# Two transformer blocks on one core: narrow weight operands laid side by side, gates and hidden layers interleaved with the queries, and three moves in VectorE's order

## The chip, the cores and the metric

One Trainium2 chip, one of its cores. The metric is the device time of one execution in microseconds (us), of which the profile covers the span from the first to the last instruction. All inputs and outputs are float32.

## The reference

Two blocks over 256 tokens of width 1024, batch 1, one after the other. What matters here is the first part of each.

```python
n = rmsnorm(h, g_mix)                       # 256 x 1024
proj = n @ w_in                             # b, c, h_conv, q, six k/v of 256 columns, g_br (48), g_conv, g_attn
k_cmp = compress(kvh(k_c), pos_k, w1_k, w2_k, n_cmp)   # n_cmp = 15 windows of 32 tokens, stride 16
v_cmp = compress(kvh(v_c), pos_v, w1_v, w2_v, n_cmp)
...
def compress(kv, pos, w1, w2, n_cmp):
    blk = kv[:, idx] + pos                  # 4 heads x 15 windows = 60 rows of 32 * 64 values
    return gelu(blk @ w1) @ w2              # 60 x 2048 by 2048 x 256, then 256 x 64
...
o = einsum('bsch,cbshd->bshd', sigmoid(g_br).reshape(B, S, 3, 16), [o_cmp, o_sel, o_win])
mix = sigmoid(g_conv) * y_conv + sigmoid(g_attn) * (o @ w_attn_out)
h = h + mix @ w_o
h = h + (silu(n @ w_gate) * (n @ w_up)) @ w_down       # D_FF = 2816
```

The second block has differential attention with a relative bias, a gated linear attention and a pooling part. Its `proj` has 16 columns `g_lr`, from which `z = g_lr @ gla_gate_w + gla_gate_b` gives the decays.

## The kernel before, in words

**Split precision.** The large matmuls take operands of type fp32r. Each operand is split in a high part (a copy by ScalarE into that type) and a low part (VectorE, operand minus high part), and a product is the sum of high by high, high by low and low by high. Activations lie in `AA` (128 partitions x 20 chunks x 2 x 256; `AH` its high and `AL` its low half). Weights come in 120 *units* of up to 1 MB (list `units`, L210 to L270).

**The ring of units.** SyncE's queue loads unit i into `RAW[i % 4]` as soon as the low part of unit i - 4 is made (L338 to L351). `hi(i)` on ScalarE (L511 to L520) writes `HI[i % 3]` in two halves, once the unit has landed and TensorE is done with unit i - 3. `lo(i)` on VectorE (L939 to L944) writes `LO[i % 3]`. TensorE waits for the halves with `unit_ready` (L1449). All four orders are written out by hand, and each engine does its instructions strictly in the order in which they stand.

**Calls of TensorE.** `stationary` (L1455 to L1473) has 128 columns of a unit as the stationary operand and 256 tokens moving: three matmuls (L1471) for each of 8 slices of 128. `both` (L1475) and `moving` (L1497) are forms for the feed-forward part and for token-major results. `take(bank, sem, value)` makes TensorE wait until the PSUM bank's last result has been read.

**First part** (L1541 to L1627). Keys, the two block units (k_c, v_c, whose results VectorE lays out as 16 slices of 60 columns, `block_sums`, split again by `block_high` and `block_low` into `BLOCKS`), the 48 gate columns (U_GATES, unit 3; `stationary` with n=48 into B[2]), four query units of two calls each (units 4 to 7), and then the hidden layers of both compressions (L1592 to L1605, units 8 to 11, three matmuls L1603 for each of 16 slices, with 60 columns). ScalarE takes the tanh of the gates from B[2] (L571) and TensorE turns them by two transposes (L1590); VectorE scales them into `GATE` (L1021). The gelu of a hidden layer runs on 60 partitions x 256: square (L589), cubic factor (L1031, L1033), tanh (L591), product (L1035), and then two transposes (L1610) and a copy into `HT` (L595). After those come the value unit 12, the products with w2 (L1617, L1622) and a small product for the relative bias (L1627).

**Attention of the first block** has 26 steps (`steps`, L281 to L288; 9 for the first 128 tokens with four heads in a step, 17 for the others with two). In step i TensorE does `scores(i)`, one or two calls of the *filler* (`FILL_AT`, L300), `turn_weights(i - 1)` (L1661) and `outputs(i - 2)` (L1698). The filler is a generator on each engine that gives the rest of the first block's projections piece by piece: a second set of keys and values, the convolution (L1110 to L1125 on VectorE), the gates of conv and attention, and the products with w_conv_out (L1138). ScalarE does `exponents(i)` (L630), the filler, `turned_weights(i - 1)` (L641), `taken` (L647). VectorE does `most(i)` (the maxima, L1062), the filler, `weights(i)` (four instructions, the last is L1083), and `taken` (L1089).

**Second block.** Unit U_TWO+4 is loaded with 128 columns, of which 16 are used (`feature_major(U_TWO + 4, 0, 1, 0)`), `LR` is copied from them (L823) and multiplied with `GW` (16 partitions, L1921). On VectorE `second_most` (L1329, L1332) waits for a turn of TensorE before its third use, and `lo(U_TWO + 9)` stands behind it (L1374, L1375). TensorE uses that unit in `rows(U_TWO + 9, ...)`, after `second_turn(1)`.

Of the kernel before, what the change touches and what calls it, by code (L numbers as in the profile page):

```python
# [6 lines left out]
F32 = mybir.dt.float32  # L7
# [3 lines left out]
ALU = mybir.AluOpType  # L11
# [48 lines left out]
def program(nc, A, out):  # L60
    with ExitStack() as ctx:
# [3 lines left out]
        def sem(name):  # L65
# [40 lines left out]
        GW = sb("GW", [16, 128])  # L106
        PW = sb("PW", [128, 2, 64])
        ROOT = sb("ROOT", [128, 8])
        hmask = sb("hmask", [128, 256])
        B = [ctx.enter_context(nc.psum_tensor(f"B{i}", [128, 512], F32)) for i in range(8)]  # L110
# [3 lines left out]
        BLOCKS = [AA[:, 12 + 4 * kv:16 + 4 * kv, :, :].rearrange("p c a n -> p (c a n)").rearrange("p (a n) -> p a n", a=2)  # L114
                  for kv in range(2)]
# [33 lines left out]
        FIRST_IN, SECOND_IN = 80, 48  # L149
# [20 lines left out]
        gates_pe, gates_tanh, gturn_pe, gates_sb = sem("gates_pe"), sem("gates_tanh"), sem("gturn_pe"), sem("gates_sb")  # L170
        q_pe, q_sb = sem("q_pe"), sem("q_sb")
        hid_pe, hid_act, hid_dve = sem("hid_pe"), sem("hid_act"), sem("hid_dve")
        hturn_pe, hturn_sb = sem("hturn_pe"), sem("hturn_sb")
# [57 lines left out]
        cols(w1, GBO, 48, gates_pe, 1)  # L231
        for u in range(4):
# [3 lines left out]
        for kv, n in enumerate(("cmp_w1_k", "cmp_w1_v")):  # L236
            for i in range(2):
                units.append((A[n][0].rearrange("(t p) n -> p t n", p=128)[:, 8 * i:8 * i + 8, :], 8, 256,
                              hid_pe, 2 * kv + i + 1))
# [21 lines left out]
        cols(w2in, 2048, 128, fm_pe, 1)  # L261
# [14 lines left out]
        U_KEYS, U_BLOCK, U_GATES, U_Q, U_HID, U_VALS = 0, 1, 3, 4, 8, 12  # L276
# [28 lines left out]

        def pieces(ring, size, i, k):

            src, nk, n, _, _ = units[i]
            if len(src.shape) == 4:
# [49 lines left out]
        def _(e):  # L359
# [22 lines left out]
            for i, n in ((47, "q_norm_g_2"), (48, "k_norm_g_2"), (50, "gla_norm_g_2")):  # L382
                for a in range(2):
# [13 lines left out]
                            pattern=[[128, 2], [-16, 32]], channel_multiplier=1).then_inc(setup, 1)  # L397
            e.memset(KC[:, :, :], 0.0).then_inc(setup, 1)
            e.memset(VB, 0.0).then_inc(setup, 1)
# [15 lines left out]
            e.dma_start(GW[:, :], A["gla_gate_w_2"][0]).then_inc(second_in, 16)  # L415
# [90 lines left out]
        def _(e):  # L506
# [55 lines left out]
            def block_high(kv, src):  # L562
                e.wait_ge(block_sb, 2 * kv + 2)
                e.activation(BLOCKS[kv][:, 0, 0:960], flatten(src[:, 0:4, :])[:, 0:960], ACT.Copy).then_inc(block_hi, 1)
# [8 lines left out]
            for u in range(4):  # L573
                c, jj = u // 2, u % 2
                if u > 0:
                    hi(U_Q + u + 2)
# [1488 lines left out]
```

## Time and profile before

| | |
|---|---|
| median of 3 runs | 765.71 us (765.52 to 767.38) |
| profiled execution, its own time | 765.83 us |
| its span | 764.1 us, 12619 instructions |
| TensorE's granted clock | 1.0 of full speed in every stretch |
| ScalarE / VectorE / GpSimd busy | 421.9 / 521.4 / 68.9 us |
| DMA | 131.78 MB, mean 172 GB/s |

Engines are named PE (TensorE matmul), PEld (its weight load, which overlaps), DVE (VectorE), ACT (ScalarE), POOL (GpSimd) and SP (SyncE). A row of a timeline has the start, the length, the engine, the line of kernel.py, the operation and its tiles, the shapes (out<-in; for a matmul, 128*48 is 128 rows by 48 columns of the stationary operand, then the moving operand), and how many instructions were merged. Matmuls are pipelined, so the length of one (0.28 us) says less than the distance between the starts of two. In brackets stands the idle time before an instruction and what ended it.

### The profile page before, as it was taken

To read this page: it belongs to the slowest core of one execution; us is meant where nothing else is said; L and a number is where in the kernel's file an instruction comes from. 1 tells how busy PE (TensorE), PEld (TensorE's weight loads), DVE (VectorE), ACT (ScalarE), POOL (GpSimd) and SP (SyncE) were. 2 spreads that over 40 slices of the span, in tenths; PEclk is the share of its full clock that TensorE was granted. 3 is DMA by queue.
4 is the path that set the end of the run, shared out by engine and by line. 5 is a ranking of instruction groups with operands and counts; after the bars stand their busy time and mean duration, and the time that the engine had idled before them with its cause. 6 is when DMAs were issued, how large, how long until landed. Compare 5 with 4: busy or idle time off the path is not lost.

```text
span 764.1 us, 12619 instructions
## 1 busy us (share of the span) xinstructions
PE 753.8 (99%) x5057; PEld 668.6 (88%) x5057; DVE 521.4 (68%) x848; ACT 421.9 (55%) x807; POOL 68.9 (9%) x106
## 2 busy tenths in 40 slices
PE   8999999999999999999999999999999999999998
PEld 7999898889899988888888888998888888888886
DVE  5857576786665767887457757888568777447762
ACT  6456656556554546555445646697645655445640
POOL 7200000001011000350000004400100000000000
PEclk9999999999999999999999999999999999999999
DMA  9978446344335556756755662843453665655611
GB/s 279 305 233 269 113 75 188 107 119 157 112 112 193 166 178 197 212 184 213 227 166 176 209 192 61 259 152 116 162 165 116 216 192 195 210 175 168 207 68 55
DMA packets 108398, 131.78 MB, mean 172 GB/s; under 512 B 4317, under 2 KB 97563, under 8 KB 108340
## 3 DMA queue, kind: packets, MB, share of 16 engines
q1 hardware_dynamic: 105780, 126.04, 52.0%
q0 software_dynamic: 2272, 4.42, 2.6%
q8 instruction: 40, 0.66, 0.4%
q10 hardware_dynamic: 288, 0.52, 0.2%
q14 instruction: 18, 0.15, 0.1%
HBM read 129.13 MB, written 1.84 MB: 171 GB/s over the span
## 4 chain that ended last, share of the span: by engine, by line
PE 83%; DVE 10%; ACT 4%; issue 2%; DMA 1%; SPq 0%; POOL 0%; ACTq 0%; DVEq 0%; POOLq 0%
PE B L1510 28%; PE B L1487 21%; PE B L1471 15%; PE B L1492 11%; DVE LO L943 3%; ACT HI L520 2%; ACT PR L630 1%; DVE SM L1062 1%; PE B L1698 1%; DVE PR L1083 1%; PE B L1651 1%; PE B L1569 1%; PE B L1661 1%; PE B L1517 1%; DMA X<-in_x 1%
## 5 line engine op out<-in xcount | busy, mean ns | idle before, releaser
L943 DVE TENSOR_TENSOR LO<-RAW,HI 128x1024 fp32r<-128x1024 f32 (+1 forms) x240 | 284.0, 1219 | 144.8 <-ACT HI L520 144.4
L520 ACT ACTIVATE HI<-RAW 128x1024 fp32r<-128x1024 f32 (+1 forms) x240 | 237.9, 1040 | 57.6 <-PE B L1510 56.8
L1487 PE MATMUL B<-AA,HI 128*128 128x512 f32 x704 | 243.3, 398 | 0.5 <-DVE AA L949 0.5
L1510 PE MATMUL B<-HI,AA 128*128 128x512 f32 (+1 forms) x832 | 217.0, 346 | 1.8 <-DVE LO L943 1.7
L1492 PE MATMUL B<-AA,LO 128*128 128x256 f32 x704 | 183.2, 281 | 0.0
L1471 PE MATMUL B<-AA,HI 128*128 128x256 f32 (+1 forms) x928 | 171.3, 286 | 0.0
L1510 PEld LDWEIGHTS B<-HI,AA 128*128 128x128 f32 x832 | 146.0, 189 | 22.1 <-issue 3.1
L1487 PEld LDWEIGHTS B<-AA,HI 128*128 128x128 f32 x704 | 126.7, 188 | 25.1 <-issue 1.1
L1471 PEld LDWEIGHTS B<-AA,HI 128*128 128x128 f32 (+1 forms) x928 | 143.7, 190 | 4.1 <-issue 2.5
L1510 PE MATMUL B<-LO,AA 128*128 128x512 f32 (+1 forms) x416 | 143.2, 344 | 0.0
L1492 PEld LDWEIGHTS B<-AA,LO 128*128 128x128 f32 x704 | 132.9, 189 | 8.2
L1471 PE MATMUL B<-AA,LO 128*128 128x256 f32 (+1 forms) x464 | 131.1, 283 | 0.0
L1471 PEld LDWEIGHTS B<-AA,LO 128*128 128x128 f32 (+1 forms) x464 | 88.2, 190 | 0.0
L1510 PEld LDWEIGHTS B<-LO,AA 128*128 128x128 f32 x416 | 78.8, 189 | 9.3
L630 ACT ACTIVATE PR<-B,SM 128x128 f32<-128x128 f32 (+1 forms) x64 | 26.2, 418 | 45.3 <-DVE SM L1062 45.3
L745 ACT ACTIVATE SGC<-SGC 128x256 f32<-128x256 f32 x44 | 16.7, 418 | 27.7 <-DVE SGC L1219 27.6
L756 ACT ACTIVATE AA<-SGC 128x256 fp32r<-128x256 f32 x44 | 16.7, 418 | 27.3 <-DVE SGC L1229 27.3
L739 ACT ACTIVATE SGC<-B 128x256 f32<-128x256 f32 x44 | 15.7, 372 | 24.1 <-PE B L1487 24.1
L750 ACT ACTIVATE SGC<-B 128x256 f32<-128x256 f32 x44 | 15.7, 371 | 20.8 <-PE B L1487 20.8
L1214 DVE TENSOR_TENSOR SGC<-B,SGC 128x256 f32<-128x256 f32 x44 | 17.7, 419 | 9.0 <-ACT SGC L739 9.0
L1224 DVE TENSOR_TENSOR SGC<-B,SGC 128x256 f32<-128x256 f32 x44 | 17.7, 419 | 5.4 <-ACT SGC L750 5.4
L1062 DVE TENSOR_REDUCE SM<-B 128x2 f32<-128x512 f32 (+1 forms) x24 | 16.4, 685 | 6.9 <-PE B L1654 6.9
(297 smaller groups left out, 624.4 us busy)
## 6 DMA issues: line engine op xcount, KB each, us to landing
RAW<-in_w_in SPq DMA_DIRECT2D x29, 1024.0 KB, 5.7
RAW<-in_w_gate SPq DMA_DIRECT2D x22, 1024.0 KB, 5.4
RAW<-in_w_up SPq DMA_DIRECT2D x22, 1024.0 KB, 5.4
RAW<-in_w_down SPq DMA_DIRECT2D x22, 1024.0 KB, 5.0
RAW<-in_w_in SPq DMA_DIRECT2D x11, 512.0 KB, 7.1
RAW<-in_w_attn_out SPq DMA_DIRECT2D x4, 1024.0 KB, 5.4
RAW<-in_w_o SPq DMA_DIRECT2D x4, 1024.0 KB, 5.0
RAW<-in_w_out SPq DMA_DIRECT2D x4, 1024.0 KB, 5.2
```

Of the source, the lines that this page charges most:

```text
L520: e.activation(pieces(HI, NSPL, i, k), pieces(RAW, NRAW, i, k), ACT.Copy).then_inc(split_hi, 1)
L630: x = e.activation(PR[:, k, j * w:j * w + w], sc[:, j, :], ACT.Exp, bias=SM[:, 3 * q, j:j + 1], accum_out=SM[:, 3 * q + 1, j:j + 1])
L745: e.activation(SGC[:, f % 4, :], SGC[:, f % 4, :], ACT.Silu).then_inc(silu_sb, 1)
L756: e.activation(AH[:, 8 + f % 12, :], SGC[:, f % 4, :], ACT.Copy).then_inc(ff_hi, 1)
L943: e.tensor_tensor(pieces(LO, NSPL, i, k), pieces(RAW, NRAW, i, k), pieces(HI, NSPL, i, k), ALU.subtract).then_inc(split_lo, 1)
L1062: e.tensor_reduce(SM[:, 3 * q, 0:n], SCORE[q][:, :].rearrange("p (j n) -> p j n", j=n), AX.X, ALU.max, negate=True).then_inc(most_sb, 1)
L1214: e.tensor_tensor(SGC[:, f % 4, :], B[c][:, 0:S], SGC[:, f % 4, :], ALU.add).then_inc(fg_sb, 1)
L1224: e.tensor_tensor(SGC[:, 4 + f % 4, :], B[5 + c][:, 0:S], SGC[:, 4 + f % 4, :], ALU.add).then_inc(fu_sb, 1)
L1471: x = e.matmul(dst, w[:, t, c0:c0 + n], a, start=(t == 0 and k == 0), stop=(t == nk - 1 and k == 2))
L1487: return e.matmul(dst[:, :], hi[:, t, c0:c0 + 128], flatten(AA[:, ch + t, :, :]), start=(t == 0), stop=(t == nk - 1))
L1492: x = e.matmul(dst[:, 0:S], lo[:, t, c0:c0 + 128], AH[:, ch + t, :], start=False, stop=False)
L1510: x = e.matmul(dst, a, w[:, t, c0:c0 + n], start=(first and t == 0 and k == 0), stop=(last and t == nk - 1 and k == 2))
```

## The change

It does the following.

- *Side by side.* For units with fewer than 64 columns (gates, 48, and U_TWO+4, now loaded with 16) the low part is written next to the high part in `HI` (64 columns apart), and `narrow` multiplies 64 + n columns with `AH` and n columns with `AL`: 16 matmuls in place of 24. `BLOCKS` has its high and low parts side by side in the same way, so a hidden layer takes two matmuls for a slice: 124 columns by the high part of w1, 60 columns by its low part.
- *Sums in the turn.* The two halves of such a result lie on different partitions. `summed_turn` multiplies by `SUMS` (two identities one above the other), which turns and adds. The gates' tanh comes after the turn, and so does the whole gelu (on 128 x 120, straight into `HT`; the factor 0.5 moves into later copies). `GW` lies twice on 80 partitions, so that its product adds the two halves.
- *Order of the first part.* The copy of the gates out of B[2] stands right behind hi(4), ahead of hi(5) and block_high(1). The hidden layers stand between the query calls, with their units in that order (q 4, 7, 10, 11; w1 5, 6 and 8, 9), and the values come last. Banks: hidden layers in B[3] and B[4], their turns in B[5] and B[6], the products with w2 in B[2] and B[7].
- *VectorE.* In attention `weights(i)` stands ahead of the filler. `lo(U_TWO + 9)` stands ahead of `second_most(2)`. `block_low(1)` stands behind lo(5) and lo(6).
- *GpSimd.* Three more memsets, one add for `SUMS`, and one more small DMA for `GW`.

```diff
@@ units
+        U_Q, U_HID = (4, 7, 10, 11), (5, 8)
...
-        cols(w2in, 2048, 128, fm_pe, 1)
+        cols(w2in, 2048, 16, fm_pe, 1)
+        def beside(i):
+            return HI[i % NSPL][:, 0:1024].rearrange("p (t a n) -> p t a n", a=2, n=64)
@@ gpsimd
+            e.memset(GW[:, :], 0.0).then_inc(pads, 1)
+            e.tensor_tensor(SUMS[:, :], ident[:, 0:64], ident[:, 64:128], ALU.add).then_inc(pads, 1)
@@ scalar
             block_high(0, SGC)
             hi(4)
+            e.wait_ge(gates_pe, 1)
+            e.activation(TMP[0:112, 0, 0:S], B[2][0:112, 0:S], ACT.Copy).then_inc(gates_act, 1)
+            hi(5)
             block_high(1, SGA)
-            hi(5)
-            e.wait_ge(gates_pe, 1)
-            e.activation(TMP[0:48, 0, 0:S], B[2][0:48, 0:S], ACT.Tanh, scale=0.5).then_inc(gates_tanh, 1)
...
+            hi(6, 0)
+            queries(0, 0)
+            hi(6, 1)
+            queries(0, 1)
+            e.wait_ge(gturn_pe, 1)
+            e.activation(GATE[:, :, :, :].rearrange("p t c h -> p (t c h)"), B[6][:, 0:96], ACT.Tanh, scale=0.5).then_inc(gates_act, 1)
+            hi(7)
+            hi(8)
+            hidden(0)
+            hi(9)
+            queries(1, 0)
+            hidden_square(0)
+            queries(1, 1)
+            hidden_tanh(0)
+            hi(10)
+            hi(11)
+            hidden(1)
...
@@ vector
             block_sums(1, SGA, 1)
-            block_low(1, SGA)
             lo(5)
             lo(6)
+            block_low(1, SGA)
             lo(7)
...
                 if i < NSTEP:
                     most(i)
+                if i < NSTEP:
+                    weights(i)
                 for _ in range(FILL_AT[i]):
                     next(filler)
-                if i < NSTEP:
-                    weights(i)
...
             second_weights(1)
+            lo(U_TWO + 9)
             second_most(2)
-            lo(U_TWO + 9)
             second_weights(2)
@@ tensor
+            def narrow(i, n, dst):
+                unit_ready(i, 1)
+                w = beside(i).rearrange("p t a n -> p t (a n)")
+                for t in range(8):
+                    if t > 0:
+                        e.matmul(dst[0:n, 0:S], w[:, t - 1, 0:n], AL[:, t - 1, :], start=False, stop=False)
+                    if t == 7:
+                        e.matmul(dst[0:n, 0:S], w[:, t, 0:n], AL[:, t, :], start=False, stop=False)
+                    x = e.matmul(dst[0:64 + n, 0:S], w[:, t, 0:64 + n], AH[:, t, :], start=(t == 0), stop=(t == 7))
+                return x
...
+                        if not last:
+                            e.matmul(B[3 + kv][0:124, 0:256], blocks[:, l, 0:124], wh[:, t, :], start=(l == 0), stop=False)
+                        x = e.matmul(B[3 + kv][0:60, 0:256], blocks[:, l, 0:60], wl[:, t, :], start=False, stop=False)
...
+            def summed_turn(dst, src, n, columns):
+                return e.matmul(dst, src[0:64 + n, columns], SUMS[0:64 + n, 0:n], start=True, stop=True)
...
+            queries(0, 0)
+            queries(0, 1)
...
+            hidden(0)
+            queries(1, 0)
+            hidden_turn(0)
+            queries(1, 1)
+            hidden(1)
+            queries(2, 0)
+            hidden_turn(1)
+            queries(2, 1)
...
+            queries(3, 0)
...
+            queries(3, 1)
+            for t in range(2):
+                values(U_VALS, 0, t)
```

## Rows read from the trace of the kernel before

**Rows 1.** The page, part 1: busy us (share of the span) and instructions of each engine.

```profile
PE 753.8 (99%) x5057; PEld 668.6 (88%) x5057; DVE 521.4 (68%) x848; ACT 421.9 (55%) x807; POOL 68.9 (9%) x106
```

**Rows 2.** The page, part 4: the chain that ended last, shares of the span.

```profile
PE 83%; DVE 10%; ACT 4%; issue 2%; DMA 1%; SPq 0%; POOL 0%; ACTq 0%; DVEq 0%; POOLq 0%
```

**Rows 3.** Waits of TensorE, whole span: total us, times, longest us.

```profile
PE B L1661 <- DVE PR L1083: 1.9, 3, 0.9
...
PE B L1510 <- DVE LO L943: 1.7, 1, 1.7
```

**Rows 4.** Timeline of TensorE, the gates' call: start, us, engine, line, operation, count.

```profile
30.49 0.28 PE L1471 MATMUL B<-AA,LO 128*128 128x256 f32 x1
...
30.62 0.40 PE L1471 MATMUL B<-AA,HI 128*48 128x256 f32 x2
...
33.37 0.40 PE L1471 MATMUL B<-AA,HI 128*128 128x256 f32 x2
```

**Rows 5.** Timeline of TensorE, first and last record of the 96 of L1603.

```profile
56.84 0.28 PE L1603 MATMUL B<-HI,AA 128*60 128x256 f32 x1
...
67.97 0.28 PE L1603 MATMUL B<-HI,AA 128*60 128x256 f32 x1
```

**Rows 6.** Timeline of TensorE, the low-rank call.

```profile
495.14 0.40 PE L1471 MATMUL B<-AA,HI 128*128 128x256 f32 x2
...
495.50 0.40 PE L1471 MATMUL B<-AA,HI 128*128 128x256 f32 x2
```

**Rows 7.** Timeline of TensorE, the gates' turns and the W2K product.

```profile
39.01 0.28 PE L1471 MATMUL B<-AA,LO 128*128 128x256 f32 x1
...
39.22 0.32 PE L1590 MATMUL B<-ident,TMP 48*128 48x48 f32 x2
...
39.81 0.28 PE L1471 MATMUL B<-AA,LO 128*128 128x256 f32 x1
...
74.90 0.55 PE L1617 MATMUL B<-HT,W2K 128*128 128x60 f32 x4
```

**Rows 8.** Busy us of each engine, stretch 30 to 40, clock, DMA share, GB/s.

```profile
30.00:40.00 10.00, 10.00 (x85) 9.81 (x84) 8.80 (x13) 4.96 (x7) 0.00 (x0) 1.00 0.91 248
```

**Rows 9.** Timeline of ScalarE and VectorE, query units, with idle before and releaser.

```profile
45.53 0.38 ACT L581 ACTIVATE QT<-B 128x256 f32<-128x256 f32 x1 [2.49 <-PE B L1471]
...
46.89 2.36 DVE L943 TENSOR_TENSOR LO<-RAW,HI 128x1024 fp32r<-128x1024 f32 x2 [2.56 <-ACT HI L520]
```

**Rows 10.** Timelines of three engines, attention steps around 115 to 122 us.

```profile
114.69 0.68 DVE L1062 TENSOR_REDUCE SM<-B 128x4 f32<-128x512 f32 x1
...
116.80 2.01 ACT L520 ACTIVATE HI<-RAW 128x1024 fp32r<-128x1024 f32 x2
...
117.90 1.23 DVE L943 TENSOR_TENSOR LO<-RAW,HI 128x1024 fp32r<-128x1024 f32 x1 [2.52 <-ACT HI L520]
...
120.89 0.69 DVE L1083 TENSOR_TENSOR PR<-PR,SM 128x512 f32<-128x512 f32 x1
...
121.50 0.68 DVE L1089 TENSOR_TENSOR AA<-B,AA 128x512 fp32r<-128x512 f32 x1
...
121.64 0.66 PE L1661 MATMUL B<-ident,PR 128*128 128x128 f32 x4 [0.86 <-DVE PR L1083]
...
122.24 0.65 PE L1698 MATMUL B<-PT,VV 128*64 128x256 f32 x4
```

**Rows 11.** Timelines of VectorE and TensorE, near 195 us.

```profile
194.52 0.41 DVE L1138 TENSOR_TENSOR SGC<-B,SGC 128x256 f32<-128x256 f32 x1
...
195.43 0.40 PE L1471 MATMUL B<-AA,HI 128*128 128x256 f32 x2
```

**Rows 12.** Timelines of VectorE and TensorE, second block, near 527 us.

```profile
524.36 0.69 DVE L1329 TENSOR_TENSOR SGC<-B,QT 128x512 f32<-128x512 f32 x1 [1.89 <-PE B L1875]
...
527.01 2.35 DVE L943 TENSOR_TENSOR LO<-RAW,HI 128x1024 fp32r<-128x1024 f32 x2
...
529.50 0.36 PE L1510 MATMUL B<-HI,AA 128*128 128x256 f32 x1 [1.72 <-DVE LO L943]
```

More of the change, by code:

```diff
@@ L1592, in _ @@
-            for kv in range(2):
-                hi, lo = BLOCKS[kv][:, 0, :], BLOCKS[kv][:, 1, :]
-                take(kv, hid_dve, 2 * kv + 2)
+            def narrow(i, n, dst):
[8 more added lines that the diff above has]
+                return x
@@ L1595, in _, with queries, hidden @@
+            take(2, gates_act, 1)
+            narrow(U_GATES, 48, B[2]).then_inc(gates_pe, 1)
+            def queries(u, k):
+                take(k, q_sb, 2 * u + k + 1)
+                stationary(U_Q[u], 128 * k, B[k][:, 0:S], 0, True).then_inc(q_pe, 1)
+            def hidden(kv):
                 e.wait_ge(block_lo, kv + 1)
+                take(3 + kv, hid_act, 3 * kv + 1)
+                blocks = BLOCKS[kv].rearrange("p l a n -> p l (a n)")
                 for half in range(2):
-                    i = U_HID + 2 * kv + half
@@ L1598, in _ @@
-                    unit_ready(i, 1)
+                    i = U_HID[kv] + half
                     wh, wl = view(HI, i), view(LO, i)
                     for t in range(8):
-                        c = slice(60 * (8 * half + t), 60 * (8 * half + t) + 60)
-                        for k, (a, w) in enumerate(((hi, wh), (hi, wl), (lo, wh))):
-                            x = e.matmul(B[kv][0:60, 0:256], a[:, c], w[:, t, :], start=(half == 0 and t == 0 and k == 0),
-                                         stop=(half == 1 and t == 7 and k == 2))
@@ L1605, in _ @@
-                    x.then_inc(hid_pe, 1)
-            for kv in range(2):
-                e.wait_ge(hid_dve, 2 * kv + 2)
-                take(5 + kv, hturn_sb, kv + 1)
+                        if t % 4 == 0:
+                            unit_ready(i, t // 4)
+                        l, last = 8 * half + t, half == 1 and t == 7
+                        if not last:
+                            e.matmul(B[3 + kv][0:124, 0:256], blocks[:, l, 0:124], wh[:, t, :], start=(l == 0), stop=False)
+                        x = e.matmul(B[3 + kv][0:60, 0:256], blocks[:, l, 0:60], wl[:, t, :], start=False, stop=False)
@@ L1614, in _ @@
+            hidden_turn(0)
+            queries(1, 1)
+            hidden(1)
+            queries(2, 0)
+            hidden_turn(1)
+            queries(2, 1)
+            e.wait_ge(hid_dve, 2)
             e.wait_ge(first_in, FIRST_IN)
-            take(0, ck_sb, 2)
+            take(2, ck_sb, 2)
             for c in range(2):
-                x = e.matmul(B[0][:, 0:60], W2K[:, c, :], HT[:, 0, c, :], start=(c == 0), stop=(c == 1))
+                x = e.matmul(B[2][:, 0:60], W2K[:, c, :], HT[:, 0, c, :], start=(c == 0), stop=(c == 1))
@@ L1624, in _ @@
             x.then_inc(cv_pe, 1)
+            queries(3, 1)
+            for t in range(2):
+                values(U_VALS, 0, t)
             e.wait_ge(setup, FAR)
@@ L1915, in _ @@
             qk_turn(0)
-            feature_major(U_TWO + 4, 0, 1, 0)
+            take(0, lr_act, 1)
+            narrow(U_TWO + 4, 16, B[0]).then_inc(fm_pe, 1)
             feature_major(U_TWO + 5, 0, 2, 4)
```

155 lines of the change are left out of this document (78 added, 77 removed).

## The prediction

> **What bounds the kernel.** I read the page's busy shares first, then its chain, the waits of TensorE, and the timelines where the diff acts. TensorE is busy for 753.8 of 764.1 us [rows 1], and the chain that ended last is 83% TensorE [rows 2]. So a matmul removed is worth its full spacing, and anything else is worth only the idle time of TensorE that it ends: 10.3 us in all, of which 1.9 us are waits of the attention turns L1661 for VectorE's weights L1083, and 1.7 us one wait of L1510 for a low part [rows 3]. VectorE and ScalarE have time to spare on average, but they run one behind the other (high part, then low part, then TensorE), so their order can still make TensorE wait.
>
> The durations are those of the profiled execution: 765.83 us, of which 764.1 are its span. The median of the runs is 765.71, so I subtract 0.1 at the end. A difference under about 0.3% (2.3 us) can't be told from none in this kernel.
>
> **1. Fewer matmuls for narrow operands.** A product costs three matmuls per slice now: high by high, high by low, low by high. The change puts the high and low parts of the narrow operand in one stationary load of 112, 80 or 124 columns; two matmuls per slice remain, one wide and one narrow, both still 256 columns long on the moving side.
> - Gates (U_GATES): the call runs from 30.62 to 33.37, 2.75 us for 24 matmuls, so 0.115 us each with 48 columns; the next call, with 128, steps by 0.12 us (0.24 for two) [rows 4].
> - Hidden layer (L1603): from 56.84 to 68.09 (the last starts at 67.97 and takes one more step), 11.25 us for 96 matmuls of 60 columns, 0.117 us each [rows 5].
> - Low rank (U_TWO+4): 24 matmuls with 128 columns. Three of its matmuls take 0.36 us (495.14 to 495.50), so 2.88 us [rows 6].
>
> Together 16.88 us for 144 matmuls. After: 16 + 64 + 16 = 96. The new wide loads of 80 to 124 columns are shown by no row; the nearest lie on both sides, 48 columns at 0.115 and 128 at 0.120 us. That gives 11.0 to 11.5 us; half of the 96 are of each kind, so I take 0.118, 11.3 us. Gain 5.5 us (5.4 to 5.9).
>
> **2. Turns that also add the two parts.** Six turns of 48 or 60 rows become ordinary f32 matmuls. Such a call leaves two records (W2K: two in the source, four records, 0.55 us together, of which about half is the length of the last, so about 0.1 us each) [rows 7]: six more records, 0.65 us. The present turns pay for something else: from the last matmul before the gates' turns (39.01) to the third after them (39.81) are 0.80 us. Three matmul steps are 0.36, so the two turns cost 0.44 us, though two records of 0.1 would be 0.2; the step before them alone is 0.21 where 0.12 is usual [rows 7]. With 112 or 124 rows that change of shape is gone, and four records of 0.1 are 0.4 us: I take 0 (-0.7 to +0.7). Likewise the one small matmul of the gates' weights with 80 rows in place of 16: -0.1.
>
> **3. The new order ahead of attention.** TensorE has no idle time here; the row for 30 to 40 us shows 10.00 of 10.00 busy [rows 8]. What is to be checked is whether splits and transfers still arrive. By the durations of the rows (high part of a unit 2.0 us, low part 2.36 us [rows 9, 10]) I walked the new order. Gates end at 32.5 in place of 33.4 and their copy, moved ahead of hi(5), holds that back until 32.9; lo(5) ends at 37.4, lo(6) at 39.8, block_low(1) at 41.0, the first half of lo(7) at 42.2. TensorE wants units 5, 6 and 7 at 38.9, 40.8 and 42.7. Unit 10 is ready at 52.3 for 52.9. So the thinnest margins are 0.4 and 0.6 us, and no wait. Of the hidden layers' chains, copy, turn, square, cubic, tanh and product, each step lies beside a query call of 2.9 us. If this cover fails, the old chain tells the price: waits of 0.1 us then, up to one split half (1.2 us) for each of two layers. Two waits of 0.1 us near 71.7 and 75.5 go: -0.2 (-0.2 to +2.4). SP's queue sees 64 KB in place of 512 KB for the low-rank unit and one small transfer more from POOL, whose memsets and add end long before 38 us: nothing. ScalarE and VectorE lose about 2 us of splits, behind TensorE: nothing.
>
> **4. Weights ahead of the fill, 26 steps.** Now VectorE does, in each step, the maxima, then the fill (which often waits for ScalarE's high part), then the weights. In the step at 114.69 the maxima end at 115.4, the exponentials at 116.80, the low part waits until 117.90, the product L1083 comes at 120.89 and TensorE starts at 121.64, after 0.86 us [rows 10]. Moved up, weights begin at 116.9 and end at 118.1, about when the low part could start anyway: in a step that begins a unit the move is free. In the next step the high part is already there; now the low part runs beside the exponentials, then it would wait for them (1.4 us, or less with two of them in place of four) and for the weights (1.2 us). Two steps cost VectorE 9.0 us before and 9.2 after: the same rate, but the fill's own products come about 2.5 us later in every second step, and these free the banks B0 and B1. Queued behind the wait are also taken(), at 121.50 now, which lets TensorE's outputs start at 122.24, and the products L1138. Walking through it: at 122.24 TensorE gains only 0.4 of the 0.86 us, since taken() ends at 121.8; the second gating product of the first round frees its bank near 126.7, 0.5 us late; the two other waits of the three [rows 3], 0.9 and 0.2 us, go. Near 195 L1138 (now at 194.52, needed by 195.43 [rows 11]) comes at 196.2 to 196.6: 1.15 us of new wait. The sum is -0.4 + 0.5 - 0.9 - 0.2 + 1.15, near zero; since TensorE's new waits give slack back to what follows, I take -0.3. Bounds: -1.9 if nothing new waits, +3 if each of the eight fills that free a bank in such a step costs 0.6 us and the old waits still go.
>
> **5. lo(U_TWO+9) ahead of second_most(2).** VectorE is idle for 1.89 us until 524.36, takes the maxima, and only then splits (527.01 to 529.36), while TensorE waits 1.72 us until 529.50 [rows 12]. The split now fits into that idle time: 522.5 to 524.8. The maxima come 0.5 us later and what they feed, the third exponentials and the high part behind them, is wanted well after 530. The wait goes: -1.7 (-1.7 to -1.2, if the copy of UP behind ScalarE is late by that 0.5).
>
> **Sum.** -5.5 - 0.1 - 0.2 - 0.3 - 1.7 = -7.8 us; 765.83 - 7.8 = 758.0, less 0.1 for the median, rounded to **758.0 us**.
>
> **A rule against part 1.** The row: going from 128 to 48 columns at 30.49 to 30.62 costs no more than a usual step, and back neither [rows 4]; going from 128 to 48 rows and back costs 0.24 us beyond the turns' own 0.2 [rows 7]. The Trainium skill, page TensorEngine Tiling (Array Packing), section Key Properties, says that a change of tiling mode, unlike a change of tile, drains TensorE. By that rule, if narrow loads counted as another mode, each alternation would pay; the trace shows it for rows and not for columns.
>
> **Rivals.**
> - *Drain at each alternation* (slower). Place: inside the two narrow calls and the two hidden layers. Wide and narrow loads alternate 14 + 14 + 30 + 30 = 88 times; at 0.12 us (half of the 0.24 above) that is 10.6 us, so 768.6. It decides from 0.09 us per change, where it eats all 7.8. Against it: the two changes of column count in [rows 4]; for it: they are two, and never alternated. This is the case that the rule of the skill describes. Chance 0.03.
> - *VectorE's new waits exceed those that go* (part 4 at its upper bound): 758.0 + 3.3 = 761.3. For it: VectorE's loop is as slow as TensorE's in the convolution steps, and banks are freed from within the fill. Chance 0.15.
> - *The move pays in full*, -1.9 in place of -0.3: 756.4. For it: TensorE's own slack may hide late banks. Chance 0.12.
> - *A split is late ahead of attention* (part 3, upper bound): 760.6. The margins of 0.4 us speak for it, the 0 us of idle now against it. Chance 0.12.
> - *The removed matmuls don't shorten the stretch*: the DMA share is 0.91 from 30 to 40 us [rows 8], and the gain of 4.5 us up to there turns into waits for units 9 to 12; only parts 4, 5 and the low-rank call remain, near 763.0. Against it: high parts waited for TensorE, 2.49 us, not for the transfer [rows 9]. Chance 0.05.
>
> **Numbers.** The forecast has 0.53. The range, 756.0 to 761.5, takes in the three neighbours with the bounds of parts 2 to 4. Faster by over 0.3%: 0.92; within: 0.05 (the rival without shortening and several late ones at once); slower: 0.03.
>
> **What would show it.** L1603's successor has 64 records over about 7.6 us, the two narrow calls 16 each over 1.9 us, steps within stay at 0.12. Scores of attention begin near 73 in place of 77.3. No wait at the call of U_TWO+9. Waits of L1661 for L1083 vanish; in their place small ones for L1089, L1123 or L1138. Wrong if steps in the narrow calls reach 0.2 us, or TensorE waits over 1 us in total between 35 and 73, or over 3 us between 75 and 225.

## The result, and the profile after

The changed kernel takes 761.76 us in the median of 13 runs (760.41 to 764.76), the kernel before 765.87 in as many (765.22 to 769.31). The ratio is 0.9943, with a 95% interval from 0.9927 to 0.996. It is faster, by 4.1 us; the forecast was 7.8 us, and the time lies 0.3 us above the range. The profiled execution took 764.64 us with a span of 762.9, so it is one of the long ones, and the spans must be taken apart before they are compared.

The page, part 1, of the changed kernel (compare [rows 1]):

```profile
PE 752.9 (99%) x5015; PEld 668.0 (88%) x5015; DVE 519.9 (68%) x848; ACT 421.4 (55%) x808; POOL 71.0 (9%) x111
```

There are 42 matmul records fewer: 48 matmuls less, six records more for the summed turns. But TensorE is busy only 0.9 us less: two stretches at half its clock, shown below, keep it busy longer. Its waits have changed as well. The waits of TensorE in the changed kernel (engine, line, releaser: total us, times, longest; compare [rows 3]):

```profile
PE B L1513 <- DVE SGC L1180: 1.9, 1, 1.9
PE B L1778 <- DVE AA L1131: 1.6, 2, 0.8
PE B L1513 <- DVE CG L1165: 1.1, 2, 0.7
```

The attention turns' waits for the weights (1.9 us) and the wait for the low part of U_TWO+9 (1.7 us) are gone. Five others stand in attention, 4.6 us together. L1180, L1131 and L1165 are the old L1138, L1089 and L1123: the gating of the products with w_conv_out, the low part of the outputs in `taken`, and the convolution's gating product.

**Cutting the span.** The transpose of VR ahead of the first block matmuls is a good zero, as TensorE's work up to it is the same in all kernels here. The tile views of that transpose, first of the kernel before and then of the changed one (its first and last start, the same for one record, stand ahead of the semicolon):

```profile
L1575 PE MATMUL B<-ident,VR x1: 260/260/260, 18.8 to 18.8; 51*128 51x51 f32 x1
```

```profile
L1617 PE MATMUL B<-ident,VR x1: 260/260/260, 21.3 to 21.3; 51*128 51x51 f32 x1
```

It comes 2.45 us later in the changed kernel's profile, for no reason of the change: by the trace's clock records TensorE's granted clock rose to full at 4.04 us there and at 12.56 us here. In the other profiles below it rose anywhere from 4.17 to 13.4 us, whichever kernel they are of. The same 26 matmuls ahead of the transpose, before and after, show what the lower clock costs:

```profile
6.18 3.17 PE L1523 MATMUL B<-ones 128*128 128x128 f32 x26
```

```profile
6.94 5.83 PE L1565 MATMUL B<-ones 128*128 128x128 f32 x26
```

(The profile's windows print 1.00 there too; the 1.0 "in every stretch" of the table before holds from the clock's rise on.) From the transpose to the end are 745.3 us before and 741.63 after. Stage by stage, by the starts of the first or last record of a kind:

| from, to | before | after | difference | forecast |
|---|---|---|---|---|
| transpose of VR, first scores | 58.46 | 53.71 | -4.76 | parts 1 to 3 without the low rank: -4.75 |
| first scores, last attention output | 156.27 | 160.42 | +4.15 | part 4: -0.3 |
| on to the second block's first q/k turn | 260.37 | 260.35 | 0 | 0 |
| on to the low-rank product with GW | 6.72 | 5.59 | -1.13 | low-rank call and GW: -1.1 |
| on to the band's first matmul | 31.91 | 29.98 | -1.93 | part 5: -1.7 |

Four stages of five are as forecast. The miss is attention.

**The side-by-side operands.** The changed kernel's lines of TensorE from 33 to 36 us, and by form from 40 to 56 us (rows by columns of the stationary operand, the moving operand, count, then busy us and mean ns):

```profile
L1632 PE MATMUL B<-AA,HI 128*112 128x256 f32 x8 | 1.9, 276 | 0.0
...
L1629 PE MATMUL B<-AA,HI 128*48 128x256 f32 x7 | 1.6, 276 | 0.0
...
L1656 PE MATMUL B<-LO,AA 128*60 128x256 f32 x32 | 7.4, 279 | 0.0
L1655 PE MATMUL B<-HI,AA 128*124 128x256 f32 x30 | 7.2, 283 | 0.0
```

All are there (the last narrow load of the gates' call and the last wide one of each hidden layer stand on lines of their own, L1631 and L1658), and no idle time in front. The timeline of the gates' call and of its turns gives the spacing:

```profile
33.06 0.28 PE L1632 MATMUL B<-AA,HI 128*112 128x256 f32 x1
33.18 0.28 PE L1629 MATMUL B<-AA,HI 128*48 128x256 f32 x1
...
34.88 0.40 PE L1513 MATMUL B<-AA,HI 128*128 128x256 f32 x2
...
40.52 0.28 PE L1513 MATMUL B<-AA,LO 128*128 128x256 f32 x1
40.64 0.54 PE L1663 MATMUL B<-SUMS,TMP 112*128 112x48 f32 x4
41.00 0.36 PE L1655 MATMUL B<-HI,AA 128*124 128x256 f32 x1
```

The call takes 1.82 us for 16 matmuls, 0.114 each, although wide and narrow loads alternate. From the last matmul before the turns (40.52) to the second after them (41.20) are 0.68 us; less two usual steps that is 0.44 for the turns, what the two old ones cost, as forecast.

**Attention.** Timeline of the changed kernel behind the weights of the step at 114 us, VectorE, ScalarE and TensorE (in brackets the idle time before the instruction and what ended it):

```profile
115.25 0.69 DVE L1125 TENSOR_TENSOR PR<-PR,SM 128x512 f32<-128x512 f32 x1
...
115.87 1.22 DVE L978 TENSOR_TENSOR LO<-RAW,HI 128x1024 fp32r<-128x1024 f32 x1
...
117.00 0.42 DVE L1165 TENSOR_TENSOR CG<-B,CG 128x256 f32<-128x256 f32 x1
...
117.45 0.42 ACT L719 ACTIVATE AA<-CG 128x256 fp32r<-128x256 f32 x1 [0.95 <-DVE CG L1165]
...
118.25 0.59 ACT L682 ACTIVATE AA<-B 128x512 fp32r<-128x512 f32 x1
...
118.87 0.69 DVE L1131 TENSOR_TENSOR AA<-B,AA 128x512 fp32r<-128x512 f32 x1 [0.55 <-ACT AA L682]
...
119.62 0.65 PE L1778 MATMUL B<-PT,VV 128*64 128x256 f32 x4 [0.76 <-DVE AA L1131]
```

The weights are ready at 115.94 and TensorE doesn't wait for them. Behind them come the low part, which starts 1.38 us after ScalarE's high part began (114.49) where it was 1.10 before [rows 10], and the convolution's product; ScalarE's high part L719 waits for that product, its copies L676 and L682 stand behind L719, `taken` (L1131) waits for L682, and TensorE's outputs wait for `taken`. The wait of [rows 10] has moved one link down, from 0.86 to 0.76 us. Counted from the first scores, the outputs start 0.3 us earlier than before (44.66 and 44.97 us). Later, in the steps with the products L1180:

```profile
192.21 0.68 DVE L1104 TENSOR_REDUCE SM<-B 128x2 f32<-128x512 f32 x1
193.98 0.17 DVE L1119 TENSOR_SCALAR SM<-SM 128x2 f32<-128x2 f32 x1 [1.09 <-ACT PR L665]
...
194.58 0.69 DVE L1125 TENSOR_TENSOR PR<-PR,SM 128x512 f32<-128x512 f32 x1
195.19 0.75 DVE L1180 TENSOR_TENSOR SGC<-B,SGC 128x256 f32<-128x256 f32 x2
```

```profile
195.66 0.50 PE L1513 MATMUL B<-AA,HI 128*128 128x256 f32 x2 [1.88 <-DVE SGC L1180]
```

VectorE sits idle for 1.09 us for the exponentials while the bank that TensorE wants could be read. ScalarE had waited for the maxima, and as long as in the kernel before; the changed kernel's row and the two of before:

```profile
192.93 0.47 ACT L665 ACTIVATE PR<-B,SM 128x256 f32<-128x256 f32 x1 [2.63 <-DVE SM L1104]
```

```profile
193.92 0.68 DVE L1062 TENSOR_REDUCE SM<-B 128x2 f32<-128x512 f32 x1
194.64 0.47 ACT L630 ACTIVATE PR<-B,SM 128x256 f32<-128x256 f32 x1 [2.67 <-DVE SM L1062]
```

Before, the product L1138 started at 194.52, 0.60 us behind the maxima and ahead of the weights [rows 11]. Now it starts 2.98 us behind them. The exponentials are hardly late: the maxima begin 1.5 us ahead of the moment at which TensorE wants the bank (195.43) in the kernel before, and 1.4 us ahead of it in the changed one (193.62, one step behind the last matmul before the wait). What is new is that the product stands behind them and the weights.

And behind this wait the clock falls. Windows of the changed kernel (length, busy us and records of PE, PEld, DVE, ACT and POOL, granted clock, DMA share, GB/s):

```profile
195.60:197.00 1.40, 1.34 (x11) 1.34 (x12) 1.40 (x3) 0.28 (x1) 0.00 (x0) 0.96 0.07 21
197.00:200.00 3.00, 3.00 (x16) 3.00 (x16) 1.63 (x3) 0.00 (x0) 0.00 (x0) 0.50 0.00 0
200.00:205.00 5.00, 5.00 (x53) 4.66 (x52) 2.63 (x7) 1.53 (x5) 0.00 (x0) 0.97 0.66 210
```

From 196.88 to 200.29 us (clock records) the granted clock is half, 1.2 in place of 2.4 GHz: 16 matmuls in 3 us.

### The profile page after: what moved, and what is told of

Read it like the earlier page. It is cut to its first block, busy times and chain, and to the rows that moved or that the text cites. A ratio compares the mean times of both kernels' runs of the same rounds, so it can differ in the third digit from the quotient of the medians.

```text
span 762.9 us, 12541 instructions
## 1 busy us (share of the span) xinstructions
PE 752.9 (99%) x5015; PEld 668.0 (88%) x5015; DVE 519.9 (68%) x848; ACT 421.4 (55%) x808; POOL 71.0 (9%) x111
## 4 chain that ended last, share of the span: by engine, by line
PE 85%; DVE 9%; ACT 3%; issue 2%; DMA 0%; SPq 0%; ACTq 0%; DVEq 0%
PE B L1552 27%; PE B L1529 21%; PE B L1513 16%; PE B L1534 11%; DVE LO L978 3%; ACT PR L665 2%; PE B L1778 1%; DVE SM L1104 1%; PE B L1731 1%; PE B L1741 1%; PE B L1611 1%; PE B L1565 1%; DVE PR L1125 1%; PE B L1559 1%; DVE CG L1157 1%
## 5 line engine op out<-in xcount | busy, mean ns | idle before, releaser
L978 DVE TENSOR_TENSOR LO<-RAW,HI 128x1024 fp32r<-128x1024 f32 x236 | 281.8, 1230 | 109.3 <-ACT HI L539 108.8
L1534 PE MATMUL B<-AA,LO 128*128 128x256 f32 x704 | 183.2, 281 | 0.0
L1513 PE MATMUL B<-AA,HI 128*128 128x256 f32 x896 | 167.7, 288 | 3.0 <-DVE SGC L1180 1.9
L1529 PEld LDWEIGHTS B<-AA,HI 128*128 128x128 f32 x704 | 126.7, 188 | 25.2 <-issue 1.1
L1513 PEld LDWEIGHTS B<-AA,HI 128*128 128x128 f32 x896 | 140.3, 192 | 7.5 <-issue 2.9
L1534 PEld LDWEIGHTS B<-AA,LO 128*128 128x128 f32 x704 | 132.9, 189 | 8.2
L1513 PE MATMUL B<-AA,LO 128*128 128x256 f32 x448 | 127.2, 284 | 0.0
L1513 PEld LDWEIGHTS B<-AA,LO 128*128 128x128 f32 x448 | 86.3, 193 | 0.0
L1119 DVE TENSOR_SCALAR SM<-SM 128x2 f32<-128x2 f32 (+2 forms) x26 | 4.4, 170 | 30.6 <-ACT PR L665 30.5
L1256 DVE TENSOR_TENSOR SGC<-B,SGC 128x256 f32<-128x256 f32 x44 | 17.7, 419 | 9.0 <-ACT SGC L774 9.0
```

What stands on the lines that cost most here:

```text
L978: e.tensor_tensor(pieces(LO, NSPL, i, k), pieces(RAW, NRAW, i, k), pieces(HI, NSPL, i, k), ALU.subtract).then_inc(split_lo, 1)
L1256: e.tensor_tensor(SGC[:, f % 4, :], B[c][:, 0:S], SGC[:, f % 4, :], ALU.add).then_inc(fg_sb, 1)
L1513: x = e.matmul(dst, w[:, t, c0:c0 + n], a, start=(t == 0 and k == 0), stop=(t == nk - 1 and k == 2))
L1529: return e.matmul(dst[:, :], hi[:, t, c0:c0 + 128], flatten(AA[:, ch + t, :, :]), start=(t == 0), stop=(t == nk - 1))
L1534: x = e.matmul(dst[:, 0:S], lo[:, t, c0:c0 + 128], AH[:, ch + t, :], start=False, stop=False)
```

## The experiments

Theory: what part 4 missed is the order of weights and filler, +2.7 us of waits in place of -0.3, and the fall of the clock behind the longest of them. Rivals: the earlier start of attention after parts 1 to 3 causes the waits; the clock falls by itself; the removed matmuls cost something in their alternation; the move could be had for nothing.

| kernel | median (range, runs) | ratio to before, 95% | transpose of VR to the end |
|---|---|---|---|
| before | 765.87 (765.22 to 769.31, 13) | 1 | 745.30 |
| changed | 761.76 (760.41 to 764.76, 13) | 0.9927 to 0.996 | 741.63 |
| e1_weights_back | 759.53 (758.3 to 760.79, 5) | 0.9896 to 0.9924 | 737.48 |
| e2_weights_alone | 769.99 (769.8 to 772.45, 6) | 1.004 to 1.0066 | 747.99 |
| e3_weights_by_unit | 757.0 (755.11 to 757.98, 4) | 0.9858 to 0.9889 | 734.93 |
| e4_back_in_three_steps | 760.03 (759.57 to 762.16, 5) | 0.9907 to 0.9934 | 738.69 |
| e5_by_unit_again | 755.37 (755.14 to 757.96, 4) | 0.9819 to 0.9868 | 734.94 |
| e6_split_back | 757.22 (757.06 to 758.85, 4) | 0.9843 to 0.9887 | 736.66 |
| e7_no_alternation | 758.12 (755.52 to 758.51, 4) | 0.984 to 0.9889 | 734.92 |
| e8_first_order_back | 756.59 (756.18 to 758.87, 5) | 0.9839 to 0.9886 | 735.77 |
| e9_changed_again | 762.69 (760.4 to 765.4, 8) | 0.9933 to 0.9968 | 741.63 |
| e10_before_by_unit | 763.95 (762.97 to 766.38, 12) | 0.9959 to 0.9985 | 742.84 |
| e11_changed_once_more | 763.67 (1) | | 741.57 |

e1 to e4 ran on one chip, e5 to e8 on a second, e9 to e11 on a third, each beside the kernel before, to which its ratio is taken. The last column, from one profile each, repeats within 0.06 us (e3 and e5; changed, e9 and e11), whereas the runs of one kernel differ by 3 us and more. Most of that is the start: the profiled executions of the changed kernel took 761.71, 763.67 and 764.64 us, and their transposes of VR stand at 18.34, 20.38 and 21.25 us. So I read the last column for every step under 2 us. The absolute times expected for the medians were missed by up to 1.7 us either way for this reason (e1 759.53 for 757 to 758.5, e2 769.99 for 768.3, e4 760.03 for 758.6, e6 757.22 for 758.7, e8 756.59 for 758.3).

**e1_weights_back.** The changed kernel with the weights behind the filler again.

```diff
             for i in range(NSTEP + 2):
                 if i < NSTEP:
                     most(i)
-                if i < NSTEP:
-                    weights(i)
                 for _ in range(FILL_AT[i]):
                     next(filler)
+                if i < NSTEP:
+                    weights(i)
```

> The changed kernel with the weights of the attention steps behind the filler again, all else kept. Theory A (the order of VectorE costs the missing gain): the waits of L1778 for taken() (1.6 us), of L1513 for the convolution's and w_conv_out's products (1.1 and 1.9 us) go, the three old waits for the weights (1.9 us) return, and the clock no longer falls to half inside attention: 757.7 us (757 to 758.5), with a spread of runs under 3 us. Rival B (the first part ends 4.8 us earlier, so attention meets the bias transfer and the weights at another point): the waits of 4.6 us stay without the order, 760.4 or more.

The cut span is 737.48 us, 7.82 less than before and 4.15 less than the changed kernel. Waits of TensorE in attention:

```profile
PE B L1741 <- DVE PR L1125: 2.0, 3, 0.9
```

The three old waits are back, the five new ones gone, the clock is full throughout. Attention takes 156.28 us, as before (156.27), so starting it 4.76 us earlier changes nothing in it. Parts 1, 2, 3 and 5 together were forecast at -7.5 and are -7.8.

**e2_weights_alone.** The kernel before, with only the weights ahead of the filler (the reverse of the diff above).

> The kernel before with the weights of the attention steps ahead of the filler, nothing else. Theory A: TensorE waits 4.6 us in attention in place of 1.9, so 2.7 us slower than before, about 768.3 us, and in some runs 1.7 us more where the clock halves after the wait near 198 us. Rival B: the order itself gains what was meant, the three waits go: 763.9 us.

```profile
PE B L1471 <- DVE SGC L1138: 1.9, 1, 1.9
PE B L1510 <- DVE LO L943: 1.7, 1, 1.7
PE B L1698 <- DVE AA L1089: 1.6, 2, 0.8
PE B L1471 <- DVE CG L1123: 1.1, 2, 0.7
```

The same five waits, each within 0.02 us, without anything else of the change: 4.6 in place of 1.9 us, +2.7, and the span between transpose and end is 2.69 us longer. In this profile the clock did not fall in attention, although the 1.9 us wait is there; one of the six executions has a mean clock of 0.998. The order of VectorE by itself makes the kernel slower (ratio 1.004 to 1.0066).

**e3_weights_by_unit.** The changed kernel with the weights ahead only in the steps whose filler begins a unit.

```diff
+                ahead = sum(FILL_AT[:i]) % 2 == 0
...
-                if i < NSTEP:
+                if i < NSTEP and ahead:
                     weights(i)
                 for _ in range(FILL_AT[i]):
                     next(filler)
+                if i < NSTEP and not ahead:
+                    weights(i)
```

> The changed kernel with the weights ahead of the filler only in steps whose first piece of filler begins a unit (its high part is not there yet), behind it in the others. Theory A: both kinds of wait go, 756.0 to 757.7 us, faster than or equal to the weights back everywhere. Rival B: 760.4 or more, as the changed kernel.

```profile
PE B L1781 <- DVE AA L1131: 0.2, 1, 0.2
```

This is the only wait left in attention. VectorE's timeline shows why:

```profile
114.14 0.17 DVE L1119 TENSOR_SCALAR SM<-SM 128x4 f32<-128x4 f32 x1 [1.57 <-ACT PR L665]
...
115.36 1.22 DVE L978 TENSOR_TENSOR LO<-RAW,HI 128x1024 fp32r<-128x1024 f32 x1
...
118.98 0.68 DVE L1104 TENSOR_REDUCE SM<-B 128x4 f32<-128x512 f32 x1
119.58 1.22 DVE L978 TENSOR_TENSOR LO<-RAW,HI 128x1024 fp32r<-128x1024 f32 x1
120.71 0.42 DVE L1165 TENSOR_TENSOR CG<-B,CG 128x256 f32<-128x256 f32 x1
```

In the step at 114 a unit begins; its high part isn't there yet, so the weights hold up the low part by only 0.3 us (it starts 1.37 us behind the start of the high part, 1.10 before). In the step at 119 the second half of the unit is ready, and the low part starts at once behind the maxima, at 119.58, with its product at 120.71. In the changed kernel the same product came at 124.09, and TensorE waited for it at 124.57. Attention takes 153.73 us, 2.5 less than before, for 1.7 us of waits less. Step by step between the kernel before and e10, where the same three waits go, each is worth 0.2 us more than its idle time: around the one of 0.86 us two steps of 1.14 and 0.17 become 0.12 and 0.11. A stop too short for the list near 149 us (0.2) goes too. It is 10.4 us less than before in the cut span, and with e5, which is the same kernel, the fastest of this study.

**e4_back_in_three_steps.** The changed kernel with the weights behind the filler only in steps 19 to 21, those of the wait for L1180.

```diff
+                ahead = i not in (19, 20, 21)
...
-                if i < NSTEP:
+                if i < NSTEP and ahead:
                     weights(i)
...
+                if i < NSTEP and not ahead:
+                    weights(i)
```

> The changed kernel with the weights behind the filler in steps 19 to 21 alone, where the products with w_conv_out lie. Theory A: the single wait of 1.9 us goes and the others (2.7 us) stay, about 758.6 us in runs with the full clock. If the halved clock (3.4 us at 197 us in the profile) follows this one wait, no run shows it any more and all lie within 1.5 us; rival: it comes with the sum of the waits or by chance, and runs up to 764 stay.

```profile
PE B L1781 <- DVE AA L1131: 1.6, 2, 0.8
PE B L1516 <- DVE CG L1165: 1.1, 2, 0.7
...
PE B L1516 <- DVE SGC L1180: 0.4, 1, 0.4
```

The waits are 3.1 us, 1.1 more than e1's 2.0, and the cut span is 1.21 longer than e1's: waits alone, no fall of the clock in this profile. Against the changed kernel it gains 2.94, of which 1.4 us are the shorter wait (1.88 to 0.45) and the rest, 1.5, the clock. The expectation that no execution would show the fall and all would lie within 1.5 us isn't met: one of the five has a mean clock of 0.998, and they spread over 2.6 us.

**e5_by_unit_again.** e3 unchanged, beside the next three.

> The same kernel as e3_weights_by_unit, for comparison with the three that follow. Theory: 757.0 again, and no stretch of the granted clock below full speed after the start-up, since no wait of TensorE in attention exceeds 0.3 us. Rival (the halved clock at 197 us in the changed kernel's profile came by itself, whatever TensorE did before): such a stretch shows here too, with about 1.6 us more.

The cut span is 734.94, e3's within 0.01. The profiled execution took 2.52 us less than e3's (755.46 and 757.98), as much as its transpose of VR comes earlier (18.79 and 21.31); the clock rose at 5.3 us, and at 12.78 in e3. That the medians differ by 1.6 us for the same reason is likely and not shown, as the other executions have no profile. There is no stretch at the lower clock between the start and the last microsecond.

**e6_split_back.** e3 with `lo(U_TWO + 9)` behind `second_most(2)` again.

```diff
-            lo(U_TWO + 9)
             second_most(2)
+            lo(U_TWO + 9)
```

> e3_weights_by_unit with lo(U_TWO + 9) behind second_most(2) again. Theory (part 5 of the prediction, a wait of 1.72 us for this low part): 1.7 us slower, near 758.7, with that wait back and the stretch from the decays' product to the band's first matmul at 31.7 to 31.9 us in place of 29.99. Rival (the wait went for another reason, for example the smaller load of the low-rank unit): no difference, 757.0.

```profile
520.73 0.36 PE L1555 MATMUL B<-HI,AA 128*128 128x256 f32 x1 [1.72 <-DVE LO L978]
```

The wait is back to the hundredth, [rows 12], and the cut span is 1.72 us longer. From the product with GW to the band's first matmul are 31.73 us, 1.75 more than in e5. Part 5 is shown alone; the smaller load of the low-rank unit had no share in it. With the split moved, a wait of 0.17 us for the copy of UP (L825) stands at the band's first matmul; in e6 it is absent.

**e7_no_alternation.** e3 with the same matmuls, all narrow ones of a call (or of a quarter of a hidden layer) in one row: 20 changes of column count in place of 88.

```diff
                 for t in range(8):
-                    if t > 0:
-                        e.matmul(dst[0:n, 0:S], w[:, t - 1, 0:n], AL[:, t - 1, :], start=False, stop=False)
...
                     x = e.matmul(dst[0:64 + n, 0:S], w[:, t, 0:64 + n], AH[:, t, :], start=(t == 0), stop=(t == 7))
+                    for s in range(8 if t == 0 else 0):
+                        e.matmul(dst[0:n, 0:S], w[:, s, 0:n], AL[:, s, :], start=False, stop=False)
```

> e3_weights_by_unit with the same matmuls in another order: in the two narrow calls and the hidden layers, all the narrow loads of a call or a quarter of a layer stand together, so that 20 changes between wide and narrow loads remain of 88. Theory (a change of the column count costs nothing): 757.0, steps of 0.114 to 0.119 us as before. Rival (each change costs something small that the forecast of 0.118 us per step hid): up to 0.5 us faster, with shorter steps.

734.92 against 734.94 us in the cut span: 68 changes less are worth nothing. (Its median is 2.8 us higher than e5's, but its profiled execution, 758.51 us, has the transpose of VR at 21.86 us, 3.07 later than e5's, where the clock rose at 13.4 us; its fastest run took 755.52.) The rival of a drain at each change is refuted, at this kind of change.

**e8_first_order_back.** e3 with the order ahead of the hidden layers as before.

```diff
             hi(4)
-            e.wait_ge(gates_pe, 1)
-            e.activation(TMP[0:112, 0, 0:S], B[2][0:112, 0:S], ACT.Copy).then_inc(gates_act, 1)
-            hi(5)
             block_high(1, SGA)
+            hi(5)
+            e.wait_ge(gates_pe, 1)
+            e.activation(TMP[0:112, 0, 0:S], B[2][0:112, 0:S], ACT.Copy).then_inc(gates_act, 1)
...
+            block_low(1, SGA)
             lo(5)
             lo(6)
-            block_low(1, SGA)
```

> e3_weights_by_unit with the kernel before's order ahead of the hidden layers: block_high(1) and hi(5) ahead of the gates' copy on ScalarE, block_low(1) ahead of lo(5) on VectorE. Theory (the new order hides the splits with margins of some 0.5 us): hi(5) then ends at 40.5 in place of 37.4 us, the gates' copy at 41.0, and the turns of the gates and units 6 and 7 are late; TensorE waits 1.0 to 1.5 us in all between 40 and 48 us, near 758.3. Rival (this part of the order is free, the low parts are early enough either way): 757.0.

0.83 us longer in the cut span, all of it ahead of the scores (54.52 us from the transpose to the first of them, 53.70 in e5). It is spread over seven longer steps from the gates' turns to the end of the first hidden layer, of which the longest stands in this timeline of TensorE:

```profile
42.62 0.28 PE L1661 MATMUL B<-HI,AA 128*124 128x256 f32 x1
43.02 0.48 PE L1516 MATMUL B<-AA,HI 128*128 128x256 f32 x2
```

A step of 0.40 us where 0.12 is usual, at the first query call behind the first hidden layer. The direction is the theory's, the size a little under its 1.0 to 1.5; in the runs' medians (756.59 and 755.37) it can't be told from the scatter of the start.

**e9_changed_again, e11_changed_once_more.** The changed kernel, profiled twice more.

> The changed kernel unchanged, for a second profile. Theory: the waits of TensorE in attention come back with the same lines and lengths (L1778 1.6, L1513 for L1165 1.1, L1513 for L1180 1.9 us), the clock's rise after the start may come anywhere from 4 to 13 us, and whether the clock is halved behind the wait near 195 us differs from execution to execution. Times near 760.4 where it isn't halved and the rise is early. Rival (the halved clock is a fixed consequence of the change): the stretch at 1.2 GHz is here again, and the best time stays above 762.

> As e9_changed_again: a third profile of the changed kernel. Theory: the waits are the same, the stretch at half clock may or may not be there. Rival: it is there each time.

The waits are the same to a tenth in both, and the cut spans 741.63 and 741.57. The clock fell in both, for 3.41 us each, at 192.87 and 194.76 us, 174.5 and 174.4 us behind the transpose, where the first profile has it at 175.6. The wait ends 174.4 us behind the transpose in all three. e9's windows of TensorE alone:

```profile
188.00:192.80 4.80, 2.92 (x25) 1.00 0.64 214
192.80:196.30 3.50, 3.50 (x17) 0.51 0.04 10
196.30:200.00 3.70, 3.70 (x43) 1.00 0.45 114
```

But it isn't there each time. Of the 22 executions of the changed kernel 12 show a mean clock of 0.996 to 0.998, and their lowest times are 761.71, 761.76 and 761.92 us; of the ten others the lowest are 760.40, 760.41 and 760.42. So the fall costs about 1.3 us where it comes. The rival of a fixed consequence is refuted by the ten executions with a mean clock of 1.000; its other sign, no time under 762, was badly chosen, as three executions with the fall lie below that. Nor does it come just anywhere: in all three profiles it starts within 1.2 us after the end of the longest wait. And it goes with the kernel: a mean clock of 0.998 or less stands in 12 of 22 executions of the changed kernel, in 1 of 6 of e2, and in 3 of 82 of those whose waits in attention are all under 1 us (one each of e4, e10 and the kernel before, 5, 12 and 39 executions). With e2 the count is too small to tell it from either. The mean doesn't say where in an execution the fall lies.

**e10_before_by_unit.** The kernel before, with e3's edit alone.

> The kernel before with the weights ahead of the filler only in the steps that begin a unit. Theory (the gain of this order is its own and doesn't need the rest of the change): the three waits of 1.9 us in attention go, about 1.9 to 2.5 us faster than before. Rival (it works in e3_weights_by_unit only because the scores start earlier against the fill's units): no gain, the waits stay.

```profile
PE B L1513 <- DVE LO L943: 1.7, 1, 1.7
...
PE B L1701 <- DVE AA L1089: 0.2, 1, 0.2
```

The three waits of 1.9 us are gone, the cut span is 2.46 us shorter, and the lowest time 762.97 against 765.25. The gain of this order is its own and adds to the rest: 2.46 in the cut span here, 2.55 between e1 and e3.

## Why the forecast missed

**Parts 1 and 2 were right.** 96 matmuls at 0.114 to 0.119 us: 1.82 us for the gates, 7.6 for the hidden layers (the first from 41.00 to 44.85), and the low-rank stage is 1.13 us shorter. The six summed turns cost what the six old ones did, 0.44 us for the gates' two.

**Part 3 was right** at -0.2 together with the rest of its stage, -4.76 for -4.75. The cover of the splits is thin, and e8 shows that the new order is part of it: 0.8 us with the old one.

**Part 5 was right.** The move is worth 1.72 us in e6's cut span. The copy of UP, of which the step had said that it might be late by 0.5 us, is late by 0.17. The stage's 1.93 us hold 0.2 more that isn't the move's: the two records of the product with GW start 0.22 us apart in place of 0.32, and 0.1 is left open.

**Part 4 is the step that failed.** "The sum is -0.4 + 0.5 - 0.9 - 0.2 + 1.15, near zero" leaves 2.05 us of waits in attention (1.9 - 0.4 - 0.9 - 0.2 + 0.5 + 1.15). There are 4.6, and e2 shows this term alone at +2.69 us, at the end of the bounds that the step gave (+3). The step between every two matmuls of attention, e2 against the kernel before, puts a number to each term (with the restart behind a wait, so these are 0.1 to 0.3 us above the idle times):

| term of part 4 | forecast | measured |
|---|---|---|
| first wait for the weights goes, outputs wait for `taken` | -0.4 | -0.25 |
| bank of the convolution's product, first round | +0.5 | +0.6 |
| second wait for the weights goes | -0.9 | -1.1 |
| the same pair of waits again in the second round | none | +1.7 |
| third wait for the weights goes | -0.2 | -0.4 |
| L1138 behind the weights | +1.15 | +2.15 |
| "slack" given back | -0.45 | not seen |

Two terms failed.

- **The second round.** The walk stopped after the first round of the convolution, where it came out: in e2 `taken` ends 44.66 us behind the first scores, which is 121.9 in the time of the kernel before (forecast 121.8), and the bank is 0.6 us late (forecast 0.5). For what followed it let the old waits go and brought no new ones. But the next unit of the convolution brings the same pair again 24 us later, in the changed kernel at 143.60 and 148.04 us (0.83 and 0.73 us idle): +1.7 where the sum has nothing.
- **The product L1138, now L1180.** "comes at 196.2 to 196.6: 1.15 us of new wait" counts from 195.43 to the start of the product. Exponentials and weights hold it back by 2.38 us (0.60 to 2.98 behind the maxima), to 196.9, and TensorE goes on only 0.47 us behind its start (195.19 to 195.66 above).

The -0.3 in place of the sum's own +0.15 rested on slack that no row shows. No run removes one of these terms alone but the last: with the old order in steps 19 to 21 (e4) the wait at L1180 shrinks from 1.88 to 0.45 us.

The rival that VectorE's new waits exceed those that go had this mechanism, with 0.15. It was priced at +3.3 against the forecast, 761.3; the waits came to +3.0 (2.69 for -0.3). The forecast and all its rivals had no term for the clock. In executions without the fall the changed kernel's lowest time is 760.4, against 765.2 before: -4.8, near the -5.1 that e1's -7.8 and e2's +2.7 make. The fall comes on top, in 5 of the 13 executions by their mean clock: the median of the eight others is 760.6 us, of all 761.76.

"Wrong if TensorE waits over 3 us between 75 and 225" was the right thing to look at, and it decides: 4.6. The rivals of a drain (e7) and of matmuls that don't shorten the stretch (first stage of the table) are refuted. The full gain of the move, put at -1.9 us, is real (-2.5) but belongs to another order, by unit (e3, e10).

## What to carry to other kernels

Before an instruction that waits is moved ahead of others on an in-order engine, ask in each step of the loop whether what it overtakes was waiting anyway; here it was in the steps that begin a unit and not in the others, and the move gains 2.5 us in the first kind alone and loses 2.7 in both. Walk every repetition, not the first round alone, and count a delay to the end of the instruction that frees the bank, not to its start. And cut the span at a point in front of the change, because the start of these executions differs by 3 us for reasons of its own, which is more than most of the steps.

## What the runs showed of the hardware

The granted clock fell to 1.2 GHz for 3.41 us in three of three profiles of the changed kernel, from 0 to 1.2 us after the end of the 1.88 us wait at L1180. In e2 TensorE has the same wait and no such stretch in the profile, and 1 of its 6 executions had a mean clock of 0.998; the wait of 1.72 us in the second block is followed by none in the profiles of the kernel before, e2, e6 and e10. So a fall follows this wait in some executions and not in others. That the wait brings it is likely from where it starts and from how rarely it comes in the kernels without the wait; it isn't shown, and what else decides isn't settled here.

At the start the clock rose to full between 4.04 and 13.4 us after the first instruction, differing between executions of the same kernel (12.56, 5.13 and 10.44 us in three of the changed one), and moved the transpose of VR between 18.3 and 21.9 us. Where two profiles of one kernel can be compared, the whole times differ by what their transposes do, to 0.1 us (2.52 us between e3 and e5, 2.93 between e9 and the first of the changed kernel), so this is likely most of the 3 to 5 us between the fastest and slowest runs of a kernel.

Stationary operands of 124 and 60 columns, or of 112 and 48, alternate at no cost (e7: 88 changes against 20, 734.94 against 734.92 us), and a wait of 0.9 us costs TensorE about 0.2 us beyond its idle time (e10).
